# In the wide stages of an fp32r kernel, h_hi and h_lo pass a loaded block of weights side by side, in one 512-column matmul

## The chip, the cores and the metric

The kernel runs on one NeuronCore of a Trainium2 chip (trn2). The metric is the device time of one execution in microseconds (us). The kernel before takes 2521.66 us, the median of 3 runs (2519.83 to 2523.13).

## The reference

The program is a whole small model in fp32 on 256 tokens of width 2048: one block with a mixer (attention, gating and an RWKV recurrence), a cross attention to a memory and a convolved feed-forward, then two layers with three kinds of attention each. What matters here are its projections, all of which are products of 256 rows `h` with a weight matrix:

```python
def hybrid_mixer(h, ...):
    z = h @ w_in                       # 2048 -> 3*768 + 2*512 + 2688 columns
    ...
def conv_ffn(h, w_up, conv_w, conv_b, w_down):
    up = h @ w_up                      # 2048 -> 2*5632
    up_pad = jnp.pad(up, ((0, 0), (CONV_WIDTH - 1, 0), (0, 0)))
    conv = conv_b + sum(up_pad[:, j:j + s] * conv_w[j] for j in range(CONV_WIDTH))
    gate, val = jnp.split(conv, 2, axis=-1)
    return (jax.nn.gelu(gate, approximate=True) * val) @ w_down
```

## The kernel before, in words

**Three products for one.** TensorE takes fp32 data in a reduced form, fp32r, which is faster than plain fp32. To keep the precision, both operands are split into a high part that fp32r holds exactly and the rest: `h = h_hi + h_lo`, `w = w_hi + w_lo`. A product is then `h_hi w_hi + h_hi w_lo + h_lo w_hi`, three matmuls that add up in one region of PSUM (`three_pass`, lines 378 to 381).

**Stages, groups, units.** Each projection is a `Stage`. It is worked in groups of 512 output columns, and a group in 4 units: a unit is 4 blocks of 128 rows of the weights by 512 columns (1 MB). SyncE loads a unit into one of four `raw` slots (`load_units`, L301 and L303). ScalarE copies it rounded into one of two `w_hi` slots (`split_hi`, L316), VectorE writes the difference into `w_lo` (`split_lo`, L321), and TensorE multiplies (`multiply`). `split_hi` of a unit waits until the unit two before it has been used (`unit_used`), and the next load into a `raw` slot waits for `lo_made`.

**Two forms.** A stage with `tok` makes the tokens the output rows: a 128x128 block of h is loaded as weights and 512 columns of w stream past it. A stage with `ch` makes the channels the output rows: a 128x128 block of w is loaded and the 256 tokens of h stream past it. For each of 4 blocks c of 128 channels and each of the unit's 4 blocks k of rows there are three matmuls of 256 columns: w_hi past h_hi (L379), then w_hi past h_lo (L380), then w_lo past h_hi (L381), 48 in a unit. In the trace the operand that streams is written first: `PS<-h_lo,w_hi` streams h_lo past w_hi. The `ch` stages that the change touches are `ST_C` (4 groups), `ST_CE` (1 group of 3 blocks of channels), `ST_UP` (22 groups, the feed-forward's first half) and the `q` stage of each of the two last layers (2 groups each). The other `ch` stages (`mem_k`, half of `bc`, `qk`, `mem_q`, half of `kv`, `c_qk`) stay as they are.

**Banks.** PSUM has 8 banks of 512 columns. A group takes two of them, and two groups in a row take different pairs. The first matmul of a group waits for the evacuation of the group two before it.

**Evacuation and what follows.** While TensorE works on a group, ScalarE and VectorE take the sums of the group before out of PSUM, right after they have split the new group's unit 1 (`evac_scalar`, `evac_vector`). In `ST_UP` the evacuation is the convolution itself: ScalarE multiplies each of 4 blocks by the tap of the same token and adds the bias, PSUM to SBUF (`up_scalar`, L1603); VectorE adds the two taps of earlier tokens, 8 instructions that read PSUM (`up_vector`, L1615). After the new group's unit 3 come the gelu (L1622) and the product with the other half (L1626). `ST_UP` is followed by `ST_DOWN`, whose stationary operand is this result (`act_ff`): its first unit needs the last group of `ST_UP` to be through all these steps and split again (L1674, L1681).

**Order.** All engines' orders are written out by hand; there is no scheduler. `ST_UP` runs in hardware loops of two groups a turn.

Of the kernel before, what the change touches and what calls it, by code (L numbers as in the profile page):

```python
# [14 lines left out]
P = 128  # L15
# [56 lines left out]
class Stage:  # L72


    def __init__(self, count, name, src, groups, tok=None, ch=None, n_cols=512, units=4, kb=4):
# [6 lines left out]
        self.scalar_end = self.vector_end = None  # L82

# [3 lines left out]
    def parity(self, g):  # L87
        return (self.G + g) % 2


# [37 lines left out]
def hybrid_two_blocks(nc, I, out):  # L128

    with ExitStack() as ctx:  # L130
        def sb(name, shape, dt=F32):
            return ctx.enter_context(nc.sbuf_tensor(name, shape, dt))
# [53 lines left out]
        def col(n):  # L186
# [13 lines left out]
        SW, SBIAS = 21248, 22272  # L200
        CONV = 16128
        cat = ar(CAT, TB, D)
# [16 lines left out]
            new(n) for n in ("hi_made", "lo_made", "unit_used", "act_evac", "dve_evac", "squared", "gained"))  # L219
        taps, gelu_made, gated_made, ff_hi, ff_lo = (  # L220
            new(n) for n in ("taps", "gelu_made", "gated", "ff_hi", "ff_lo"))
        (mem_in, consts_in, rel_in, rel_out, rel_back, x_in, sgu_in, masks_in, lora_in, g_up_in, ln_in, gains_in,
# [7 lines left out]
        def w_cols(w, col0, stride=512, n_cols=512):  # L230
# [10 lines left out]
        ST_BC = Stage(count, "bc", w_cols(w_in, 3 * A_W + 768), 1, tok=(0, 256), ch=(256, 256))  # L241
        ST_C = Stage(count, "c", w_cols(w_in, C0 + 256), 4, ch=(0, 512))
        ST_CE = Stage(count, "c_end", w_cols(w_in, C0 + 256 + 2048, n_cols=384), 1, ch=(0, 384), n_cols=384)
        ST_VB = Stage(count, "vb", w_cols(w_in, 2 * A_W + 512), 1, tok=(0, 512))
# [6 lines left out]
        ST_UP = Stage(count, "ffn_up", lambda g, j: tuple(w_up[:, 4 * j:4 * j + 4, bass.ds(g * S + a, S)]  # L251
                                                          for a in (0, D_FF)), FB // 2, ch=(0, 512))
        ST_DOWN = Stage(count, "ffn_down", lambda q, j: w_down[:, bass.ds(q * 4 + j, 1), :], FB // 4, kb=1, n_cols=2048)
        count["group"] = ST_DOWN.G
        ST2 = []
        for layer in range(LAYERS):
            w = I["w_in_2"][layer]
            ST2.append(dict(
                q=Stage(count, "q", w_cols(w, 0), 2, ch=(0, 512)),
                kv=Stage(count, "kv", w_cols(w, 1024), 1, tok=(256, 256), ch=(0, 256)),  # L260
                tok=Stage(count, "tok", w_cols(w, 1536), 4, tok=(0, 512)),
                tok_end=Stage(count, "tok_end", w_cols(w, 3584, n_cols=192), 1, tok=(0, 192), n_cols=192),
                c_qk=Stage(count, "c_qk", w_cols(w, 3776), 2, ch=(0, 512)),
                c_vg=Stage(count, "c_vg", w_cols(w, 4800), 2, tok=(0, 512)),
                out=Stage(count, "w_out_2", w_cols(I["w_out_2"][layer], 0), 4, tok=(0, 512))))
# [66 lines left out]
        def group_scalar(act, q, before=None, made=0):  # L332
            st = q.st
            for j in range(st.units):
                if j >= made:
                    split_hi(act, q, j)
                if j == min(1, st.units - 1) and before is not None:
                    evac_scalar(act, before)
                yield
            if before is not None and before.st.scalar_end:  # L340
                before.st.scalar_end(act, before)

        def group_vector(dve, q, before=None, made=0):
            st = q.st
            for j in range(st.units):
                if j >= made:
                    split_lo(dve, q, j)
                if j == min(1, st.units - 1) and before is not None:
                    evac_vector(dve, before)
                yield  # L350
            if before is not None and before.st.vector_end:
                before.st.vector_end(dve, before)

        def last_scalar(act, q):
            evac_scalar(act, q)
# [82 lines left out]
        def to_tokens(st, dst, col0):  # L438
            plain_evac(st, lambda g: dst[:, 0, bass.ds(g * 512 + col0, 512)],
                       lambda g: dst[:, 1, bass.ds(g * 512 + col0, 512)])  # L440

        def to_channels(st, at, blk0):
            plain_evac(st, lambda g: arena[:, bass.ds(g * 1024 + (at + blk0 * S), 512)],
                       lambda g: arena[:, bass.ds(g * 1024 + (at + blk0 * S + 512), 512)])
# [11 lines left out]
        to_channels(ST_C, Z_C, 2)  # L456
        plain_evac(ST_CE, lambda g: ar(Z_C + 18 * S, 512), lambda g: ar(Z_C + 20 * S, 256))

# [1132 lines left out]
        act_ff = ar(0, FB * S)  # L1591
        conv = ar(CONV, 2, 4, S)

# [4 lines left out]
        def up_scalar(act, q):  # L1598
            if q.c >= 2:
                act.wait_ge(gated_made, q.plus(2, q.c - 1))  # L1600
            for m in range(4):
                half, c = m // 2, m % 2
                last = act.activation(conv[:, q.parity, m, :], PS[:, 2 * q.parity + half, c * S:(c + 1) * S], ACT.Identity,  # L1603
                                      scale=channel("conv_w", q.g, half, c, 2), bias=channel("conv_b", q.g, half, c))
            last.then_inc(act_evac, 1)

        def up_vector(dve, q):
            dve.wait_ge(act_evac, q.number(1))
            for back in (1, 2):
                if back == 2:  # L1610
                    dve.wait_ge(taps, q.plus(2, q.c + 1))
# [6 lines left out]
                last.then_inc(taps if back == 1 else dve_evac, 1)  # L1618

        def gate_scalar(act, q):  # L1620
            act.wait_ge(dve_evac, q.number(1))
            act.activation(conv[:, q.parity, 0:2, :], conv[:, q.parity, 0:2, :], ACT.Gelu_apprx_tanh).then_inc(gelu_made, 1)  # L1622

        def gate_vector(dve, q):
# [1026 lines left out]
```

## Time and profile before

| | |
|---|---|
| runs | 2519.83, 2521.66, 2523.13 us |
| the profiled execution's own time | 2520.95 us |
| its span, first to last instruction | 2519.2 us |
| TensorE (matmul) busy | 2316.0 us, 92% of the span, 14998 matmuls |
| VectorE busy | 1324.6 us, 53% |
| ScalarE busy | 1020.8 us, 41% |
| mean granted TensorE clock | 0.954 of full speed |
| share of TensorE in the chain that ended last | 87% |

A matmul's busy time in the profile (284 ns for 256 columns) is from its start to the modelled end of its pipeline, and the next one starts before that. What a matmul costs in a stream is the distance between two starts, read in the timeline, or the length of a stretch over the number of matmuls in it.

### The profile page before, as it was taken

The page shows a single profiled execution, that of the slowest core. Times are in us where ns is not written, and L with a number is a line of the kernel's source. Part 1 is how long each engine was busy: PE and PEld are TensorE (multiplying, and loading weights), DVE is VectorE, ACT ScalarE, POOL GpSimd, SP SyncE. Part 2 cuts the span into 40 slices and gives each one's busy share as a digit, 9 for nine tenths or more (in the row PEclk, how much of TensorE's full clock was granted, in tenths as well). Part 3 has the DMA queues.
Part 4 walks back from the last instruction along what each step waited for, and adds up shares of the span by engine and source line. Part 5 has one row for each costly group of instructions (what it writes and reads, how often), then busy time and mean ns, then how long its engine had stood idle before and what let it go on. Part 6 is the DMA issues. An engine that isn't in the chain of part 4 may idle for free.

```text
span 2519.2 us, 35800 instructions
## 1 busy us (share of the span) xinstructions
PE 2316.0 (92%) x14998; PEld 2097.8 (83%) x14998; DVE 1324.6 (53%) x1675; ACT 1020.8 (41%) x1303; POOL 44.4 (2%) x55
## 2 busy tenths in 40 slices
PE   7999987978888899999998999799998999999897
PEld 6898976867766899999997888698976779898676
DVE  5444645375555655555554554644455554444654
ACT  4433432322444544444443344433444343343542
POOL 0000010010000000000000000000000000000000
PEclk9999987979899999999999999899998999999898
DMA  7456520000643455555554555364640446555033
GB/s 283 153 170 213 182 78 1 1 1 11 227 164 101 150 184 181 181 181 181 181 198 161 188 199 187 129 224 156 206 134 1 151 159 221 183 186 167 1 122 129
DMA packets 217831, 373.12 MB, mean 148 GB/s; under 512 B 8263, under 2 KB 108020, under 8 KB 210804
## 3 DMA queue, kind: packets, MB, share of 16 engines
q1 hardware_dynamic: 211088, 360.48, 42.7%
q10 hardware_dynamic: 6628, 10.98, 1.2%
q8 instruction: 87, 1.43, 0.2%
q14 instruction: 28, 0.23, 0.0%
HBM read 369.32 MB, written 2.12 MB: 147 GB/s over the span
## 4 chain that ended last, share of the span: by engine, by line
PE 87%; DVE 8%; ACT 3%; DMA 1%; issue 1%; POOL 0%; ACTq 0%; DVEq 0%; SPq 0%
PE PS L379 25%; PE PS L381 25%; PE PS L380 25%; PE PS L1509 2%; PE PS L996 1%; DVE w_lo L321 1%; PE PS L1493 1%; PE PS L1003 1%; DVE small L1546 1%; ACT w_hi L316 1%; DVE spare L1542 1%; PE PS L574 1%; PE PS L1332 1%; PE PS L1331 1%; DVE x L659 1%
## 5 line engine op out<-in xcount | busy, mean ns | idle before, releaser
L321 DVE TENSOR_TENSOR w_lo<-raw,w_hi 128x2048 fp32r<-128x2048 f32 (+2 forms) x340 | 766.4, 2254 | 786.7 <-ACT w_hi L316 784.7
L316 ACT ACTIVATE w_hi<-raw 128x2048 fp32r<-128x2048 f32 (+2 forms) x340 | 640.3, 1883 | 772.3 <-PE PS L381 755.3
L379 PE MATMUL PS<-h_hi,w_hi 128*128 128x256 f32 x2640 | 750.3, 284 | 5.8 <-DVE w_lo L321 3.6
L381 PE MATMUL PS<-h_hi,w_lo 128*128 128x256 f32 x2640 | 747.9, 283 | 0.0
L380 PE MATMUL PS<-h_lo,w_hi 128*128 128x256 f32 x2640 | 747.9, 283 | 0.0
L379 PE MATMUL PS<-w_hi,h_hi 128*128 128x512 f32 (+2 forms) x1440 | 551.4, 383 | 35.1 <-DVE h_lo L596 12.0
L381 PE MATMUL PS<-w_hi,h_lo 128*128 128x512 f32 (+2 forms) x1440 | 548.1, 381 | 0.0
L380 PE MATMUL PS<-w_lo,h_hi 128*128 128x512 f32 (+2 forms) x1440 | 548.0, 381 | 0.0
L379 PEld LDWEIGHTS PS<-h_hi,w_hi 128*128 128x128 f32 x2640 | 507.2, 192 | 7.7 <-issue 3.9
L380 PEld LDWEIGHTS PS<-h_lo,w_hi 128*128 128x128 f32 x2640 | 507.3, 192 | 0.0
L381 PEld LDWEIGHTS PS<-h_hi,w_lo 128*128 128x128 f32 x2640 | 507.2, 192 | 0.0
L379 PEld LDWEIGHTS PS<-w_hi,h_hi 128*128 128x128 f32 x1440 | 274.7, 191 | 87.5 <-issue 18.9
L381 PEld LDWEIGHTS PS<-w_hi,h_lo 128*128 128x128 f32 x1440 | 274.2, 190 | 50.9
L380 PEld LDWEIGHTS PS<-w_lo,h_hi 128*128 128x128 f32 x1440 | 274.5, 191 | 50.1
L574 PE MATMUL PS<-ident,arena 128*128 128x128 f32 x296 | 46.9, 319 | 63.7 <-ACT arena L533 36.8
L574 PEld LDWEIGHTS PS<-ident,arena 128*128 128x128 f32 x296 | 42.0, 168 | 68.2 <-issue 36.0
L1615 DVE SCALAR_TENSOR_TENSOR arena<-PS,params,arena 128x255 f32<-128x255 f32 (+1 forms) x176 | 72.6, 474 | 6.2 <-ACT arena L1603 3.5
L1674 ACT ACTIVATE h_hi<-arena 128x256 fp32r (+1 forms) x44 | 18.3, 418 | 139.5 <-PE PS L381 138.8
L581 ACT ACTIVATE h_hi<-PS,params 128x256 fp32r<-128x256 f32 x106 | 42.4, 474 | 62.9 <-PE PS L574 62.7
L525 POOL TENSOR_TENSOR small<-small 128x2 f32<-128x2 f32 (+2 forms) x31 | 27.2, 885 | 2035.9 <-DVE small L656 955.2
L591 DVE SCALAR_TENSOR_TENSOR h_lo<-PS,params,h_hi 128x256 fp32r<-128x256 f32 x106 | 43.8, 476 | 33.1 <-ACT h_hi L581 33.1
L1681 DVE TENSOR_TENSOR h_lo<-arena,h_hi 128x256 fp32r<-128x256 f32 x44 | 18.6, 425 | 64.2 <-ACT h_hi L1674 64.2
(466 smaller groups left out, 1652.3 us busy)
## 6 DMA issues: line engine op xcount, KB each, us to landing
raw<-in_w_in SPq DMA_DIRECT2D x132, 1024.0 KB, 5.1
raw<-in_ffn_w_up SPq DMA_DIRECT2D x176, 512.0 KB, 4.3
raw<-in_w_out SPq DMA_DIRECT2D x48, 1024.0 KB, 5.1
raw<-in_ffn_w_down SPq DMA_DIRECT2D x44, 1024.0 KB, 4.7
raw<-in_mem_wkv SPq DMA_DIRECT2D x8, 1024.0 KB, 7.2
raw<-in_mem_wq SPq DMA_DIRECT2D x4, 1024.0 KB, 5.1
raw<-in_mem_wo SPq DMA_DIRECT2D x4, 1024.0 KB, 5.5
raw<-in_w_in SPq DMA_DIRECT2D x4, 768.0 KB, 4.5
```

Of the source, the lines that this page charges most:

```text
L316: act.activation(w_hi[:, slot % 2, :st.n], raw[:, slot, :st.n], ACT.Copy).then_inc(hi_made, 1)
L321: dve.tensor_tensor(w_lo[:, slot % 2, :st.n], raw[:, slot, :st.n], w_hi[:, slot % 2, :st.n].bitcast(F32), ALU.subtract).then_inc(lo_made, 1)
L379: pe.matmul(ps, l_hi, r_hi, start=start, stop=False, skip_group_check=skip)
L380: pe.matmul(ps, l_hi, r_lo, start=False, stop=False, skip_group_check=skip)
L381: return pe.matmul(ps, l_lo, r_hi, start=False, stop=stop, skip_group_check=skip)
L525: return pool.tensor_tensor(c, c, minus_half.to_broadcast([P, n]), ALU.pow)
L574: last = pe.transpose(PS[:, turn_bank(n), at:at + P], block(t, k), ident[:, :])
L581: act.activation(h_hi[:, k, :], PS[:, turn_bank(n), (k % 2) * S:(k % 2 + 1) * S], ACT.Copy, scale=gain(k)).then_inc(j.act, 1)
L591: dve.scalar_tensor_tensor(out=h_lo[:, k, :], in0=PS[:, turn_bank(n), (k % 2) * S:(k % 2 + 1) * S], scalar=gain(k), in1=h_hi[:, k, :].bitc ...
L659: dve.scalar_tensor_tensor(out=x[:, tb, :], in0=y[:, tb, :], scalar=j.rstd[:, tb:tb + 1], in1=x[:, tb, :], op0=ALU.mult, op1=ALU.add).then ...
L1509: last = pe.matmul(PS[:, bank, t_ * P:(t_ + 1) * P], s_[:, (kb * TB + t_) * P:(kb * TB + t_ + 1) * P], job["v"][:, kb, :], start=kb == 0, ...
L1615: last = dve.scalar_tensor_tensor(out=d, in0=PS[:, 2 * q.parity + half, c * S:(c + 1) * S - back], scalar=channel("conv_w", q.g, half, c, ...
```

## The change

For the stages with the new argument `wide`, one matmul streams h_hi and h_lo, 256 columns each, past a block of w_hi. Its 512 results fill one PSUM bank: `h_hi w_hi` in the left half, `h_lo w_hi` in the right half. The matmul with w_lo adds into the left half. A unit's block of channels has its four wide matmuls first, then its four with w_lo. For this h_hi and h_lo become two halves of one tensor `h_both`, a group takes four banks (0 to 3 or 4 to 7 in turn), and the evacuation adds the halves: ScalarE copies the left halves of the banks to SBUF, and VectorE adds the right halves to them in place. In `ST_UP` the sums land in a new buffer `rows_up`, and the convolution reads that, one unit later (`scalar_mid`, `vector_mid`, after unit 2).

```diff
-        h_hi = sb("h_hi", [P, KB, S], F32R)
-        h_lo = sb("h_lo", [P, KB, S], F32R)
+        h_both = sb("h_both", [P, 2, KB, S], F32R)
+        h_hi, h_lo = h_both[:, 0], h_both[:, 1]
...
+    def wide_bank(self, g):
+        return (self.wide + 4 * g) % 8
...
+        ST_C = Stage(..., ch=(0, 512), wide=4)
+        ST_CE = Stage(..., ch=(0, 384), n_cols=384, wide=4)
+        ST_UP = Stage(..., ch=(0, 512), wide=0)
+                q=Stage(count, "q", w_cols(w, 0), 2, ch=(0, 512), wide=0),
...
@@ group_scalar (group_vector alike)
                 if j == min(1, st.units - 1) and before is not None:
                     evac_scalar(act, before)
+                if j == 2 and before is not None and before.st.scalar_mid:
+                    before.st.scalar_mid(act, before)
@@ multiply
-                pe.wait_ge(act_evac, q.number(-1))
-                pe.wait_ge(dve_evac, q.number(-1))
+                late = 0 if st.wide == 0 and q.c == 0 and q.i is None else -1
+                pe.wait_ge(act_evac, q.number(late))
+                pe.wait_ge(dve_evac, q.number(late))
...
-            if st.ch:
+            if st.wide is not None:
+                c0, n = st.ch
+                for c in range(n // P):
+                    cs = slice(c0 + c * P, c0 + (c + 1) * P)
+                    sums = PS[:, q.bank + c, :].rearrange("p (a n) -> p a n", a=2)
+                    for k in range(st.kb):
+                        kk = j * st.kb + k
+                        pe.matmul(sums, wh[:, k, cs], h_both[:, :, kk, :], start=kk == 0, stop=False, skip_group_check=True)
+                    for k in range(st.kb):
+                        kk = j * st.kb + k
+                        last = pe.matmul(sums[:, 0, :], wl[:, k, cs], h_hi[:, kk, :], start=False, stop=kk == end,
+                                         skip_group_check=True)
+            elif st.ch:
@@ evacuation of ST_C, ST_CE and q
+        def wide_sums(q, half, c0=0, n=4):
+            return PS[:, q.bank + c0:q.bank + c0 + n, half * S:(half + 1) * S]
+        def wide_evac(st, dst):
+            n = st.ch[1] // P
+            def scalar(act, q):
+                act.activation(blocks_in(dst(q.g), n), wide_sums(q, 0, 0, n), ACT.Copy).then_inc(act_evac, 1)
+            def vector(dve, q):
+                d = blocks_in(dst(q.g), n)
+                dve.wait_ge(act_evac, q.number(1))
+                dve.tensor_tensor(d, d, wide_sums(q, 1, 0, n), ALU.add).then_inc(dve_evac, 1)
@@ evacuation and convolution of ST_UP
         def up_scalar(act, q):
             if q.c >= 2:
                 act.wait_ge(gated_made, q.plus(2, q.c - 1))
+            act.activation(rows_up[:, q.parity, :, :], wide_sums(q, 0), ACT.Copy).then_inc(act_evac, 1)
+
+        def up_vector(dve, q):
+            dve.wait_ge(act_evac, q.number(1))
+            up = rows_up[:, q.parity, :, :]
+            dve.tensor_tensor(up, up, wide_sums(q, 1), ALU.add).then_inc(dve_evac, 1)
+
+        def conv_scalar(act, q):
+            act.wait_ge(dve_evac, q.number(1))
             for m in range(4):
-                last = act.activation(conv[...], PS[:, 2 * q.parity + half, c * S:(c + 1) * S], ACT.Identity,
+                last = act.activation(conv[...], rows_up[:, q.parity, m, :], ACT.Identity,
...
-            last.then_inc(act_evac, 1)
+            last.then_inc(first_tap, 1)
+        def conv_vector(dve, q):
+            dve.wait_ge(first_tap, q.plus(2, q.c + 1))
...
-                    last = dve.scalar_tensor_tensor(out=d, in0=PS[:, 2 * q.parity + half, c * S:(c + 1) * S - back],
+                    last = dve.scalar_tensor_tensor(out=d, in0=rows_up[:, q.parity, m, :S - back],
...
         def gate_scalar(act, q):
-            act.wait_ge(dve_evac, q.number(1))
+            act.wait_ge(taps, q.plus(4, 2 * q.c + 2))
```

How the instructions move, at three places. First TensorE at the start of a unit in the loop of `ST_UP`, before:

```order
3574 L388 ISA
3575 L379 MATMUL PS<-h_hi,w_hi 128x256
3576 L380 MATMUL PS<-h_lo,w_hi 128x256
3577 L381 MATMUL PS<-h_hi,w_lo 128x256
3578 L379 MATMUL PS<-h_hi,w_hi 128x256
```

and of the change (L428 is the wide matmul, L431 the one with w_lo):

```order
2654 L406 ISA
2655 L428 MATMUL PS<-h_both,w_hi 128x512 x4
2656 L431 MATMUL PS<-h_both,w_lo 128x256 x4
2657 L428 MATMUL PS<-h_both,w_hi 128x512 x4
2658 L431 MATMUL PS<-h_both,w_lo 128x256 x4
```

A unit's 48 matmuls of 256 columns (16 times the three lines) have become 16 of 512 and 16 of 256 columns.

Second ScalarE from the first group of `ST_UP` into the second, before (L316 is `split_hi`, L1603 the convolution out of PSUM, L1622 the gelu):

```order
299 L316 ACTIVATE w_hi<-raw 128x2048 x3
300 L1603 ACTIVATE arena<-PS,params 128x256 x4
301 L316 ACTIVATE w_hi<-raw 128x2048 x2
302 L1622 ACT_TABLE_LOAD
303 L1622 ACTIVATE arena<-arena 128x512
```

and of the change (L325 is `split_hi`, L1654 the copy out of PSUM, L1665 the convolution from SBUF, L1684 the gelu):

```order
299 L325 ACTIVATE w_hi<-raw 128x2048 x3
300 L1654 ACTIVATE arena<-PS 128x1024
301 L325 ACTIVATE w_hi<-raw 128x2048
302 L1665 ACTIVATE arena<-arena,params 128x256 x4
303 L325 ACTIVATE w_hi<-raw 128x2048
304 L1684 ACT_TABLE_LOAD
305 L1684 ACTIVATE arena<-arena 128x512
```

The convolution has moved behind one more split, and a copy of 1024 columns stands in its place.

Third ScalarE at the end of `ST_UP`, where nothing lies between the steps, before:

```order
356 L316 ACTIVATE w_hi<-raw 128x2048
357 L1603 ACTIVATE arena<-PS,params 128x256 x4
358 L1622 ACTIVATE arena<-arena 128x512
359 L1674 ACTIVATE h_hi<-arena 128x256 x2
```

and of the change:

```order
366 L325 ACTIVATE w_hi<-raw 128x2048
367 L1654 ACTIVATE arena<-PS 128x1024
368 L1665 ACTIVATE arena<-arena,params 128x256 x4
369 L1684 ACTIVATE arena<-arena 128x512
370 L1737 ACTIVATE h_both<-arena 128x256 x2
```

The chain from the last matmul of `ST_UP` to the first of `ST_DOWN` has one more link on ScalarE, and VectorE has one more too (its addition of 1024 columns, before its 8 taps).

## Rows read from the trace of the kernel before

**Rows 1.** The page: busy shares and the chain that ended last, by engine and line.

```profile
PE 2316.0 (92%) x14998; PEld 2097.8 (83%) x14998; DVE 1324.6 (53%) x1675; ACT 1020.8 (41%) x1303; POOL 44.4 (2%) x55
PE 87%; DVE 8%; ACT 3%; DMA 1%; issue 1%; POOL 0%; ACTq 0%; DVEq 0%; SPq 0%
```

**Rows 2.** Busy us (count) by engine, clock, DMA share, GB/s: ST_C/ST_CE, ST_UP, ST_DOWN, tok.

```profile
99.50:211.70 112.20, 112.20 (x937) 112.20 (x936) 48.02 (x26) 39.03 (x25) 0.00 (x0) 1.00 0.56 183
843.60:1338.90 495.30, 495.30 (x4130) 495.30 (x4129) 278.93 (x279) 216.44 (x196) 0.00 (x0) 1.00 0.56 184
...
1347.30:1589.00 241.70, 241.70 (x1055) 199.96 (x1056) 116.46 (x86) 94.73 (x85) 0.00 (x0) 0.99 0.53 187
...
1681.20:1768.25 87.05, 87.05 (x386) 72.11 (x385) 37.74 (x20) 31.51 (x20) 0.00 (x0) 1.00 0.53 170
```

**Rows 3.** Timeline (start us, us) of TensorE in ST_UP, 256 columns each.

```profile
1000.18 0.28 PE L381 MATMUL PS<-h_hi,w_lo 128*128 128x256 f32 x1
1000.30 0.28 PE L379 MATMUL PS<-h_hi,w_hi 128*128 128x256 f32 x1
1000.42 0.28 PE L380 MATMUL PS<-h_lo,w_hi 128*128 128x256 f32 x1
1000.54 0.28 PE L381 MATMUL PS<-h_hi,w_lo 128*128 128x256 f32 x1
```

**Rows 4.** Timeline of TensorE in a tok stage, 512 then 192 columns each.

```profile
1700.25 0.39 PE L379 MATMUL PS<-w_hi,h_hi 128*128 128x512 f32 x1
1700.48 0.39 PE L380 MATMUL PS<-w_lo,h_hi 128*128 128x512 f32 x1
...
1768.56 0.27 PE L379 MATMUL PS<-w_hi,h_hi 128*128 128x192 f32 x1
...
1768.90 0.27 PE L379 MATMUL PS<-w_hi,h_hi 128*128 128x192 f32 x1
```

**Rows 5.** ScalarE and VectorE through one group of ST_UP (timeline).

```profile
1206.79 1.91 ACT L316 ACTIVATE w_hi<-raw 128x2048 fp32r<-128x2048 f32 x1 [2.03 <-PE PS L381]
...
1205.18 3.44 DVE L1615 SCALAR_TENSOR_TENSOR arena<-PS,params,arena 128x255 f32<-128x255 f32 x8
1208.73 2.29 DVE L321 TENSOR_TENSOR w_lo<-raw,w_hi 128x2048 fp32r<-128x2048 f32 x1
1214.49 2.29 DVE L321 TENSOR_TENSOR w_lo<-raw,w_hi 128x2048 fp32r<-128x2048 f32 x1 [3.47 <-ACT w_hi L316]
```

**Rows 6.** Groups by form: two of 1024 or 512 columns on ScalarE and VectorE.

```profile
L1859 ACT ACTIVATE arena<-arena 128x1024 f32<-128x1024 f32 x6 | 6.3, 1047 | 0.0
L1818 DVE TENSOR_TENSOR x<-x,PS 128x512 f32<-128x512 f32 x8 | 5.5, 683 | 12.0 <-PE PS L381 12.0
```

**Rows 7.** The chain of waits from the last matmul of ST_UP to ST_DOWN's first.

```profile
1339.11 0.13 PE PS L381
1339.26 1.94 ACT arena L1603 x4
1341.29 1.66 DVE arena L1615 x4
1342.98 1.66 DVE arena L1615 x4
1344.67 0.64 ACT arena L1622
1345.33 0.70 DVE arena L1626
1346.06 0.43 ACT h_hi L1674
1346.57 0.44 DVE h_lo L1681
1347.01 0.25 issue
1347.26 0.76 PE PS L379
```

**Rows 8.** Stretches as in rows 2: the start of ST_DOWN, and a plain fp32 matmul (L2101).

```profile
1347.30:1352.60 5.30, 5.30 (x13) 4.14 (x14) 2.33 (x2) 1.28 (x1) 0.00 (x0) 0.50 0.14 20
...
1920.90:1924.30 3.40, 3.40 (x6) 1.37 (x5) 0.00 (x0) 2.95 (x7) 0.00 (x0) 0.50 0.00 0
```

**Rows 9.** Plain fp32 matmuls: L2101 in the timeline, then the lines L2101 and L2089 (ns min/median/max).

```profile
1920.92 3.62 PE L2101 MATMUL PS<-arena 128*128 128x512 f32 x4
...
L2101 PE MATMUL PS<-arena x16: 592/878/1062, 1920.9 to 2385.2; 128*128 128x512 f32 x16
...
L2089 PE MATMUL PS<-arena x80: 378/380/635, 1882.8 to 2364.0; 128*128 128x256 f32 x80
```

More of the change, by code:

```diff
@@ L72, with __init__ @@
 class Stage:
-    def __init__(self, count, name, src, groups, tok=None, ch=None, n_cols=512, units=4, kb=4):
+    def __init__(self, count, name, src, groups, tok=None, ch=None, n_cols=512, units=4, kb=4,
+                 wide=None):
         self.name, self.src, self.groups, self.tok, self.ch = name, src, groups, tok, ch
@@ L81, in __init__ @@
         self.U1, self.G1 = count["unit"], count["group"]
-        self.scalar_end = self.vector_end = None
+        self.wide = wide
+        self.scalar_mid = self.vector_mid = self.scalar_end = self.vector_end = None
     def unit(self, g):
@@ L219, in hybrid_two_blocks @@
             new(n) for n in ("hi_made", "lo_made", "unit_used", "act_evac", "dve_evac", "squared", "gained"))
-        taps, gelu_made, gated_made, ff_hi, ff_lo = (
-            new(n) for n in ("taps", "gelu_made", "gated", "ff_hi", "ff_lo"))
+        first_tap, taps, gelu_made, gated_made, ff_hi, ff_lo = (
+            new(n) for n in ("first_tap", "taps", "gelu_made", "gated", "ff_hi", "ff_lo"))
         (mem_in, consts_in, rel_in, rel_out, rel_back, x_in, sgu_in, masks_in, lora_in, g_up_in, ln_in, gains_in,
@@ L241, in hybrid_two_blocks @@
         ST_BC = Stage(count, "bc", w_cols(w_in, 3 * A_W + 768), 1, tok=(0, 256), ch=(256, 256))
-        ST_C = Stage(count, "c", w_cols(w_in, C0 + 256), 4, ch=(0, 512))
-        ST_CE = Stage(count, "c_end", w_cols(w_in, C0 + 256 + 2048, n_cols=384), 1, ch=(0, 384), n_cols=384)
+        ST_C = Stage(count, "c", w_cols(w_in, C0 + 256), 4, ch=(0, 512), wide=4)
+        ST_CE = Stage(count, "c_end", w_cols(w_in, C0 + 256 + 2048, n_cols=384), 1, ch=(0, 384), n_cols=384,
+                      wide=4)
         ST_VB = Stage(count, "vb", w_cols(w_in, 2 * A_W + 512), 1, tok=(0, 512))
@@ L251, in hybrid_two_blocks @@
         ST_UP = Stage(count, "ffn_up", lambda g, j: tuple(w_up[:, 4 * j:4 * j + 4, bass.ds(g * S + a, S)]
-                                                          for a in (0, D_FF)), FB // 2, ch=(0, 512))
+                                                          for a in (0, D_FF)), FB // 2, ch=(0, 512), wide=0)
         ST_DOWN = Stage(count, "ffn_down", lambda q, j: w_down[:, bass.ds(q * 4 + j, 1), :], FB // 4, kb=1, n_cols=2048)
@@ L349, in group_vector @@
                     evac_vector(dve, before)
+                if j == 2 and before is not None and before.st.vector_mid:
+                    before.st.vector_mid(dve, before)
                 yield
@@ L402, in multiply @@
                                           kk == end, at_once)
-            if st.ch:
+            if st.wide is not None:
+                c0, n = st.ch
[10 more added lines that the diff above has]
+            elif st.ch:
                 c0, n = st.ch
@@ L456, in hybrid_two_blocks @@
         to_channels(ST_C, Z_C, 2)
-        plain_evac(ST_CE, lambda g: ar(Z_C + 18 * S, 512), lambda g: ar(Z_C + 20 * S, 256))
+        wide_evac(ST_CE, lambda g: ar(Z_C + 18 * S, 768))
         def vb_scalar(act, q):
@@ L1600, in up_scalar @@
                 act.wait_ge(gated_made, q.plus(2, q.c - 1))
+            act.activation(rows_up[:, q.parity, :, :], wide_sums(q, 0), ACT.Copy).then_inc(act_evac, 1)
[5 more added lines that the diff above has]
+            act.wait_ge(dve_evac, q.number(1))
             for m in range(4):
                 half, c = m // 2, m % 2
-                last = act.activation(conv[:, q.parity, m, :], PS[:, 2 * q.parity + half, c * S:(c + 1) * S], ACT.Identity,
+                last = act.activation(conv[:, q.parity, m, :], rows_up[:, q.parity, m, :], ACT.Identity,
                                       scale=channel("conv_w", q.g, half, c, 2), bias=channel("conv_b", q.g, half, c))
-            last.then_inc(act_evac, 1)
-        def up_vector(dve, q):
-            dve.wait_ge(act_evac, q.number(1))
+            last.then_inc(first_tap, 1)
+        def conv_vector(dve, q):
+            dve.wait_ge(first_tap, q.plus(2, q.c + 1))
             for back in (1, 2):
                 if back == 2:
-                    dve.wait_ge(taps, q.plus(2, q.c + 1))
+                    dve.wait_ge(taps, q.plus(4, 2 * q.c + 1))
                 for m in range(4):
@@ L1614, in up_vector @@
                     d = conv[:, q.parity, m, back:]
[L1615 removed]
+                    last = dve.scalar_tensor_tensor(out=d, in0=rows_up[:, q.parity, m, :S - back],
                                                     scalar=channel("conv_w", q.g, half, c, 2 - back), in1=d, op0=ALU.mult,
                                                     op1=ALU.add)
[L1618 removed]
+                last.then_inc(taps, 1)
         def gate_scalar(act, q):
[L1621 removed]
+            act.wait_ge(taps, q.plus(4, 2 * q.c + 2))
             act.activation(conv[:, q.parity, 0:2, :], conv[:, q.parity, 0:2, :], ACT.Gelu_apprx_tanh).then_inc(gelu_made, 1)
@@ L1629, in hybrid_two_blocks @@
         ST_UP.scalar_evac, ST_UP.vector_evac = up_scalar, up_vector
+        ST_UP.scalar_mid, ST_UP.vector_mid = conv_scalar, conv_vector
         ST_UP.scalar_end, ST_UP.vector_end = gate_scalar, gate_vector
```

16 lines of the change are left out of this document (13 added, 3 removed).

## The prediction, made before the change was run

> **What bounds the kernel now.** I read the page first: TensorE is busy 92% of the span, and 87% of the chain that ended last is its own work [rows 1]. So a gain has to come out of TensorE's stream, and what the other engines do costs only where TensorE waits for it. Next I cut the span into stages. In `ST_C` with `ST_CE` and in `ST_UP` TensorE is busy in every microsecond at the full clock (1.00), VectorE 43 to 56% and ScalarE 35 to 44% [rows 2]. There is no wait to remove; only the matmuls themselves can become cheaper. Then the timeline, for what one matmul costs, from start to start: the busy figure of 0.28 us overlaps the next matmul and is not the price. With 256 columns the starts are 120 ns apart [rows 3]; over the whole of `ST_UP`, 495.30 us for 22 x 4 x 48 = 4224 matmuls less the two units' 96 of its opening, 4128, gives 119.99 ns. With 512 columns they are 227 ns apart [rows 4]; over 16 units of 24 matmuls, 87.05 / 384 = 226.7 ns [rows 2].
>
> From 256 to 512 columns the price rises by 106.7 ns, which is 256 columns at 2.4 GHz. So both have the same fixed part: 120.0 - 106.7 = 13.3 ns and 226.7 - 213.3 = 13.4 ns. With 192 columns the starts are (1768.90 - 1768.56) / 3 = 113 ns apart [rows 4], 33 ns over the 80 ns of its columns: below 256 columns another floor shows, at about 111 to 113 ns. The new stream has nothing under 256 columns, so that floor stays out of it.
>
> **The matmuls.** The number of columns stays: 3 x 256 before, 512 + 256 after. What goes is one matmul of three, with its weight load, and so one fixed part. Per pair (block of channels c, block of rows k): before 3 x 120.0 = 360.0 ns, after 226.7 + 120.0 = 346.7 ns, 13.3 ns less. Pairs: `ST_C` 4 groups x 4 units x 16 = 256; `ST_CE` 4 x 12 = 48; `ST_UP` 22 x 4 x 16 = 1408; the two q stages 2 x 2 x 4 x 16 = 256. Together 1968 pairs x 13.3 ns = 26.2 us.
>
> The Trainium skill (TensorE: Matmul & The Clock Gate, "Back-to-back issue gap") gives a matmul N / 2.4 ns plus about 2.5 ns at the warm clock. By that a dropped matmul would be worth 2.5 ns, 4.9 us in all, and the kernel would come to about 2519. The trace has 13.3 ns for the fixed part of fp32r matmuls with a weight load each, at both lengths, and the sum goes by the trace.
>
> **The wide matmul's operand.** No fp32r matmul before streams its operand in two pieces (256 columns of h_hi, then 256 of h_lo 16 KB further on). The nearest row is L2101, in plain fp32, which streams 4 pieces of 128 columns, 256 apart (`ukv4[:, k, :, P:2P]`). At the half clock its four matmuls fill 3.62 us, of which the last one's 1.06 us: (3.62 - 1.06) / 3 = 853 ns each [rows 8, 9], exactly 2 x 512 columns at 1.2 GHz. At the full clock its shortest is 592 ns against 378 ns for L2089, which streams 256 columns in one piece [rows 9]: 214 ns for 256 more columns at two steps a column, again nothing for the pieces. Plain fp32 takes two steps a column, though, so a cost of a piece could hide in it. Bounds: 0 from this row; 33 ns, from the 192-column row, if the second piece behaved like a short matmul; below 0 nothing, since no row shows a 512-column matmul under 227. I take 0, the nearest row's.
>
> **The supply of a unit.** A unit of `ST_UP` shrinks from 48 x 0.12 = 5.76 us to 16 x 0.3467 = 5.55 us. Splitting it takes 1.91 + 2.29 us one after the other, started when the unit before the one running is used up [rows 5]; TensorE needs it 5.55 us later, so some 1.2 us are left. The extra work goes into that: after unit 1 ScalarE copies 1024 columns, 1.05 us by L1859 [rows 6], and VectorE adds 1024, which lies between 683 ns for 512 columns [rows 6] and 2290 ns for 2048 [rows 5], so about 1.22 us. Behind ScalarE's copy stands only the split of unit 2, due at 5.55 us, and ScalarE is done at 3.0 us; VectorE is done at 1.94 + 2.29 + 1.22 = 5.45 us, and its next split can start only at 5.55 + 1.94. After unit 2 VectorE's split ends at 4.2 us and ScalarE's four convolution steps at 1.91 + 1.94 = 3.85 us [rows 5, 7]; the 8 taps, 3.44 us [rows 5], run to 7.65 us, and the split of unit 3 that is queued behind them could have started at 7.49. It is 0.16 us late, ends at 9.9, and is needed at 11.1. Cover stays, and TensorE doesn't wait. SyncE's next load, which waits for that split, slips by the same 0.16 us of a three-unit lead. The loads rise from 184 to 191 GB/s, against 187 in `ST_DOWN`, which is busy throughout as well [rows 2]. In `ST_C` and q the copy and the addition are the same and nothing follows them.
>
> The waits on evacuated banks have the same distance of two groups; the `late` wait at the head of `ST_UP` and q is for a group whose sums the opening itself already needed. Both at 0.
>
> **Where it costs.** At the end of `ST_UP` nothing covers. From 1339.11 to 1347.26 us TensorE waits for ScalarE's convolution, VectorE's taps, gelu, product and split, 8.15 us [rows 7]. The change puts the copy (1.05) and the addition (1.22) in front: +2.3 us, all on the path. The taps from SBUF rather than PSUM I leave at their price. After the gap the clock is at 0.50 for the first 5.3 us of `ST_DOWN` [rows 8], which costs 2.65 us; where in the idle time the clock falls and returns differs from gap to gap, so this and the other gaps can move the end by about 2 us either way. At the hand-over from `ST_CE` the split is late already and a unit shorter by 0.16 us adds 0.16. In three openings a split is made in between transposes; I allow 0.2 us in all.
>
> **Sum.** 26.2 - 2.3 - 0.16 - 0.2 = 23.5 us. The profiled execution took 2520.95 us, so 2497.4; that execution lies 0.7 us under the median, which gives 2498.2. I say 2498 us.
>
> **Rivals.**
> *Each piece pays.* If the fixed 13.3 ns belongs to a run of columns and not to a matmul, the wide one takes 240 ns, the pair 360, nothing is gained and the longer tail stays: 2521.7 + 2.7 = 2524. For it: no fp32r row in pieces. Against: L2101 in four pieces. A measurement of this kernel tells 0.2%, 5 us, from no change, so this reads as no change. 0.10.
>
> *A break between the pieces costs more* (the slower side). The price is the short matmul's: 33 ns a wide matmul, so the pair takes 380 ns, 19.7 ns more than now, x 1968 = +38.8, with the tail 2563 us. It loses by 5 us from 14.5 ns a break on ((13.3 x 1968 + 2300) / 1968). Against it speaks the same row L2101, whose 853 ns leave room for 0 ns. 0.06. The Trainium skill (Advanced Engine Details and Errata, "PSUM Cachelines") says that any non-contiguous access pattern slows matmuls significantly, and would put this rival first; but it also says that two neighbours suffice, and here the PSUM side is one run of 512 and the SBUF side runs of 1 KB. L2101's rows disagree with the sweeping form.
>
> *Half comes through.* The break between the pieces costs half of a fixed part, 6.65 ns x 1968 = 13.1 us, or a waiting split inside `ST_UP` gives back as much (0.15 us in each of its 88 units): 2511. For it: the unseen operand, and VectorE's fuller queue. Against: the 1.2 us of cover. 0.07.
>
> *More comes off.* If the fixed part is a clash of a weight load with the stream that a thinner sequence avoids, every matmul of the pair drops to its columns: 213.3 + 106.7 = 320, 40 ns a pair, 79 us, 2445. Against: the 512-column stream has weight loads just as thin and pays 13.4 ns. 0.05.
>
> Forecast 0.72. Its own range, from the clock's 2 us and 1 ns a pair: 2493 to 2504. The range of 8 in 10 takes in the half case: 2490 to 2512. Faster by over 0.2% (under 2516.6): 0.72 + 0.07 + 0.05 = 0.84; within: 0.10; slower: 0.06.
>
> **What would show it.** In the changed profile: starts 227 ns after a wide matmul and 120 ns after one with w_lo; a group of `ST_UP` in 22.2 us instead of 23.05, so the stage 18.7 us shorter; `ST_C` with `ST_CE` 4.0 us shorter; each q stage 1.7; about 10.4 us of idle TensorE before `ST_DOWN` instead of 8.15; no wait for w_lo inside `ST_UP`. I am wrong if the distance after a wide matmul is not 227, or if TensorE shows waits for VectorE in the loop.

## The result and the profile after

The changed kernel takes 2508.13 us (median of 5 runs, 2502.02 to 2510.02) against 2520.63 us before (5 runs, 2519.83 to 2523.13): ratio 0.9939, 95% interval 0.9925 to 0.9954. It is faster by 12.5 us, about half of the 23.5 us that were forecast. It lies in the stated range (2490 to 2512), but outside the forecast's own one (2493 to 2504).

The page of the changed kernel, in the form of [rows 1]:

```profile
PE 2299.9 (92%) x13030; PEld 1994.4 (80%) x13030; DVE 1353.4 (54%) x1697; ACT 1050.4 (42%) x1325; POOL 44.4 (2%) x55
PE 86%; DVE 9%; ACT 3%; DMA 1%; issue 1%; POOL 0%; ACTq 0%; DVEq 0%; SPq 0%
```

1968 matmuls are gone from the 14998, and TensorE bounds the kernel as before. The same stretches as in [rows 2] and [rows 8]: `ST_C` with `ST_CE`; the loop of `ST_UP`; the wait before `ST_DOWN`; `c_qk` of both layers; the start of `ST_DOWN`. The first line can't be set against that of [rows 2] as it stands: the window there also holds 24 matmuls of the stage before `ST_C`, 2.9 us.

```profile
103.90:210.55 106.65, 106.65 (x610) 93.17 (x608) 48.54 (x25) 40.72 (x25) 0.00 (x0) 1.00 0.58 187
841.68:1324.55 482.87, 482.87 (x2755) 421.97 (x2753) 302.06 (x300) 241.20 (x217) 0.00 (x0) 1.00 0.58 189
1324.55:1335.23 10.68, 0.17 (x2) 0.03 (x1) 5.93 (x12) 4.93 (x9) 0.00 (x0) 0.63 0.30 98
1767.84:1816.11 48.27, 48.27 (x391) 48.27 (x392) 22.54 (x25) 22.38 (x24) 1.39 (x2) 0.97 0.53 175
2221.03:2269.39 48.36, 48.36 (x391) 48.36 (x392) 22.54 (x25) 22.38 (x24) 1.39 (x2) 0.96 0.53 174
1335.23:1341.00 5.77, 5.77 (x14) 4.51 (x15) 2.37 (x2) 1.32 (x1) 0.00 (x0) 0.50 0.10 23
```

The loop of `ST_UP` is 86 units, 1376 pairs: 482.87 / 1376 = 350.9 ns a pair where 346.7 were expected and 360.0 stood before (the other two units of the 88 are worked in the stage's opening). TensorE is busy in all of it, so the missing 4 ns are not a wait. The timeline of the changed kernel in that loop shows where they are (start us, us of the merged matmuls):

```profile
1000.39 1.09 PE L428 MATMUL PS<-h_both,w_hi 128*128 128x512 f32 x4
1001.32 0.64 PE L431 MATMUL PS<-h_both,w_lo 128*128 128x256 f32 x4
1001.79 0.40 PE L428 MATMUL PS<-h_both,w_hi 128*128 128x512 f32 x1
```

Four wide matmuls fill 1001.32 - 1000.39 = 0.93 us, 232.5 ns each; four with w_lo 0.47 us, 117.5 each. Over that loop, mean from start to start: a wide one followed by a wide one 233.6 ns, a wide one followed by a w_lo one 228.4, a w_lo one 118.5. (Over the whole trace the first is 234.4, with the stages' openings in it; the texts on the experiments below use that.) A pure stream of 512 columns had 226.7 [rows 2], a pure one of 256 had 120.0.

From span to span (2519.2 to 2507.8, 11.4 us less): `ST_UP` 12.65 less, `ST_C` and `ST_CE` 2.8, the q stages 1.1 each, together 17.7; the wait before `ST_DOWN` 2.5 more; `c_qk` 1.4 and 1.5 more, where the changed kernel's clock is at half for about 3.4 us and before's was not; 0.9 more in the other gaps and restarts together. Of the 12.1 us that these 11.4 fall short of the 23.5 forecast, 8.5 are the matmuls, 2.9 the clock in `c_qk`, 0.2 the wait before `ST_DOWN` and 0.5 the rest.

### The profile page after: what moved, and what is told of

Its sections match the earlier page's. It is cut to its first block, busy times and chain, and to the rows that moved or that the text cites. A ratio compares the mean times of both kernels' runs of the same rounds, so it can differ in the third digit from the quotient of the medians.

```text
span 2507.8 us, 31953 instructions
## 1 busy us (share of the span) xinstructions
PE 2299.9 (92%) x13030; PEld 1994.4 (80%) x13030; DVE 1353.4 (54%) x1697; ACT 1050.4 (42%) x1325; POOL 44.4 (2%) x55
## 4 chain that ended last, share of the span: by engine, by line
PE 86%; DVE 9%; ACT 3%; DMA 1%; issue 1%; POOL 0%; ACTq 0%; DVEq 0%; SPq 0%
PE PS L428 18%; PE PS L396 16%; PE PS L397 16%; PE PS L398 16%; PE PS L431 9%; PE PS L1562 2%; DVE w_lo L330 1%; PE PS L1049 1%; PE PS L1546 1%; DVE small L1599 1%; ACT w_hi L325 1%; PE PS L1056 1%; DVE spare L1595 1%; PE PS L627 1%; PE PS L1385 1%
## 5 line engine op out<-in xcount | busy, mean ns | idle before, releaser
L325 ACT ACTIVATE w_hi<-raw 128x2048 fp32r<-128x2048 f32 (+2 forms) x340 | 640.6, 1884 | 728.6 <-PE PS L398 369.8
L396 PE MATMUL PS<-w_hi,h_both 128*128 128x512 f32 (+2 forms) x1440 | 551.6, 383 | 38.6 <-DVE h_both L649 12.0
L397 PE MATMUL PS<-w_lo,h_both 128*128 128x512 f32 (+2 forms) x1440 | 548.4, 381 | 0.0
L398 PE MATMUL PS<-w_hi,h_both 128*128 128x512 f32 (+2 forms) x1440 | 548.3, 381 | 0.0
L428 PE MATMUL PS<-h_both,w_hi 128*128 128x512 f32 x1968 | 538.3, 395 | 1.5 <-DVE h_both L644 1.5
L428 PEld LDWEIGHTS PS<-h_both,w_hi 128*128 128x128 f32 x1968 | 336.5, 189 | 47.5 <-DVE h_both L644 2.4
L396 PEld LDWEIGHTS PS<-w_hi,h_both 128*128 128x128 f32 x1440 | 275.1, 191 | 91.1 <-issue 22.4
L431 PEld LDWEIGHTS PS<-h_both,w_lo 128*128 128x128 f32 x1968 | 302.0, 189 | 41.9
L398 PEld LDWEIGHTS PS<-w_hi,h_both 128*128 128x128 f32 x1440 | 274.6, 191 | 51.5
L397 PEld LDWEIGHTS PS<-w_lo,h_both 128*128 128x128 f32 x1440 | 274.9, 191 | 50.0
L431 PE MATMUL PS<-h_both,w_lo 128*128 128x256 f32 x1968 | 313.0, 281 | 0.0
L396 PE MATMUL PS<-h_both,w_hi 128*128 128x256 f32 x672 | 193.4, 288 | 4.1 <-DVE w_lo L330 3.6
L397 PE MATMUL PS<-h_both,w_hi 128*128 128x256 f32 x672 | 191.7, 285 | 0.0
L398 PE MATMUL PS<-h_both,w_lo 128*128 128x256 f32 x672 | 191.6, 285 | 0.0
L396 PEld LDWEIGHTS PS<-h_both,w_hi 128*128 128x128 f32 x672 | 130.6, 194 | 5.2 <-issue 3.9
L397 PEld LDWEIGHTS PS<-h_both,w_hi 128*128 128x128 f32 x672 | 130.5, 194 | 0.0
L398 PEld LDWEIGHTS PS<-h_both,w_lo 128*128 128x128 f32 x672 | 130.5, 194 | 0.0
L1677 DVE SCALAR_TENSOR_TENSOR arena<-arena,params 128x255 f32<-128x255 f32 (+1 forms) x176 | 73.2, 478 | 4.9 <-ACT arena L1665 2.1
```

The costliest lines, as they stand in the source:

```text
L325: act.activation(w_hi[:, slot % 2, :st.n], raw[:, slot, :st.n], ACT.Copy).then_inc(hi_made, 1)
L396: pe.matmul(ps, l_hi, r_hi, start=start, stop=False, skip_group_check=skip)
L397: pe.matmul(ps, l_hi, r_lo, start=False, stop=False, skip_group_check=skip)
L398: return pe.matmul(ps, l_lo, r_hi, start=False, stop=stop, skip_group_check=skip)
L428: pe.matmul(sums, wh[:, k, cs], h_both[:, :, kk, :], start=kk == 0, stop=False, skip_group_check=True)
L431: last = pe.matmul(sums[:, 0, :], wl[:, k, cs], h_hi[:, kk, :], start=False, stop=kk == end, skip_group_check=True)
```

## The experiments

**Is it the two pieces, the order or the bank?** The first theory was the break in the streamed operand, the prediction's own doubt. The rivals: the order (a wide matmul right behind a wide one) and the shared PSUM bank.

e1, h_hi and h_lo of a block side by side:

```diff
-        h_both = sb("h_both", [P, 2, KB, S], F32R)
-        h_hi, h_lo = h_both[:, 0], h_both[:, 1]
+        h_both = sb("h_both", [P, KB, 2, S], F32R)
+        h_hi, h_lo = h_both[:, :, 0, :], h_both[:, :, 1, :]
```

The wide matmul, and the instructions that fill h_both, address it accordingly.

> The layout alone: h_both is [KB, 2, S] instead of [2, KB, S], so that h_hi and h_lo of one block of rows lie side by side and the wide matmul streams 512 columns in one piece. Order as in the change (four wide, then four w_lo). In the profile of the change a wide matmul that a wide one follows takes 234.4 ns and one that a w_lo one follows 228.4 ns; w_lo ones 118.5 ns. Theory A (a break in the streamed operand costs about 7 ns): wide to wide falls to 227, a block's eight matmuls from 1405 to about 1382 ns, ST_UP is 352 x 0.023 = 8 us shorter, 2500 us. Theory B (it is the order: a wide matmul right behind a wide one): wide to wide stays at 234, time as the change, 2508 us.

e2, one loop over k instead of two:

```diff
                         pe.matmul(sums, wh[:, k, cs], h_both[:, :, kk, :], ...)
-                    for k in range(st.kb):
-                        kk = j * st.kb + k
                         last = pe.matmul(sums[:, 0, :], wl[:, k, cs], h_hi[:, kk, :], ...)
```

> The order alone: in each block of channels wide, w_lo, wide, w_lo, ... for the four k, layout as in the change (two pieces). Theory B: no wide matmul follows a wide one, so the pair takes 228.4 + 118.4 = 346.8 ns, 4.6 ns less than the change's 351.4; over 1968 pairs 9 us, 2499 us. Theory A: each wide matmul keeps its break, 234 + 119 = 353 ns a pair, time as the change or 3 us above it, 2508 to 2511 us.

e3, both edits:

> Layout of e1 and order of e2 together. Both theories: 227 + 119 to 120 = 346 to 347 ns a pair, about 2499 us. If each of the two has a part of its own, this one is faster than either alone.

e4, k outside, blocks of channels inside:

```diff
+                for k in range(st.kb):
+                    kk = j * st.kb + k
+                    for c in range(n // P):
+                        cs, sums = block(c)
+                        pe.matmul(sums, wh[:, k, cs], h_both[:, :, kk, :], ...)
+                    for c in range(n // P):
+                        cs, sums = block(c)
+                        last = pe.matmul(sums[:, 0, :], wl[:, k, cs], h_hi[:, kk, :], ...)
```

> Layout as in the change, the order within a unit turned: k outside, blocks of channels inside, so for each k four wide matmuls into four different PSUM banks, then four w_lo ones into the four banks. The share of wide matmuls that follow a wide one is as in the change. Theory C (two wide matmuls in a row into the same PSUM bank cost 7 ns): wide to wide falls to 227 or 228, about 2500 us. Theories A and B: stays at 234, about 2508 us.

All three theories fell. The loop of `ST_UP` in e1, in e2, in e3 and in e4:

```profile
841.47:1324.35 482.88, 482.88 (x2755) 421.94 (x2753) 302.14 (x300) 241.12 (x217) 0.00 (x0) 1.00 0.58 189
...
837.66:1323.94 486.28, 486.28 (x2755) 421.60 (x2753) 302.87 (x300) 241.29 (x217) 0.00 (x0) 1.00 0.57 188
...
837.61:1323.90 486.29, 486.29 (x2755) 421.45 (x2753) 302.88 (x300) 241.31 (x217) 0.00 (x0) 1.00 0.57 188
...
841.73:1324.62 482.89, 482.89 (x2755) 421.94 (x2753) 302.11 (x300) 241.22 (x217) 0.00 (x0) 1.00 0.58 189
```

In one piece the loop takes 482.88 us, as in two (482.87): the break is free. Alternating, it is 3.4 us longer, 353.4 ns a pair: a wide matmul then takes 236.5 ns and a w_lo one 116.9. Both edits together (e3) are as e2. With four banks (e4) the loop is as the change's, and wide to wide stays at 233.6 in it. As whole kernels: e1 2510.13 us (ratio 0.9947, 0.9934 to 0.996), e2 2509.05 (0.9943, 0.9928 to 0.9958), e3 2508.42 (0.9948, 0.9935 to 0.9961), e4 2510.78 (0.9953, 0.9938 to 0.9967); their intervals overlap the change's.

**Is it the mixture of lengths or the roles?** What the four had in common was 512- and 256-column matmuls in one stream (theory D), and weights of w under a stream of 512 columns of h (theory E).

e5, no short matmul left in the wide stages:

```diff
-                        last = pe.matmul(sums[:, 0, :], wl[:, k, cs], h_hi[:, kk, :], start=False, ...)
+                        last = pe.matmul(sums, wl[:, k, cs], h_both[:, :, kk, :], start=False, ...)
```

> The change with the w_lo matmul wide as well: it streams h_hi and h_lo past w_lo, so the fourth product h_lo w_lo is added into the right half of the sums, which the reference's precision doesn't need. No 256-column matmul is left in the wide stages. Theory D (the 7 ns come from long and short matmuls in one stream): all starts are 227 apart as in the tok stages, 454 ns a pair, ST_UP 1408 x 0.454 = 639 us. Theory E (they come from the roles: weights of w loaded, 512 columns of h streamed): all starts 234 apart, 468 ns a pair, ST_UP 659 us. Whole kernel 2508 + 1968 x 0.103 to 0.117 = 2711 to 2738 us.

e6, a unit's 16 wide matmuls, then its 16 short ones:

```diff
                 for c in range(n // P):
...
                     for k in range(st.kb):
...
                         pe.matmul(sums, wh[:, k, cs], h_both[:, :, kk, :], ...)
+                for c in range(n // P):
...
                     for k in range(st.kb):
...
                         last = pe.matmul(sums[:, 0, :], wl[:, k, cs], h_hi[:, kk, :], ...)
```

> A unit's 16 wide matmuls first (all four blocks of channels), then its 16 with w_lo: one change of length a unit instead of four. In the change wide to wide is 234.4 ns, wide to w_lo 228.4, w_lo 118.5. Theory D: long runs come near the pure streams, 227 and 120, 347.5 ns a pair, ST_UP 489 us. Theory E: 15 x 234.4 + 228.4 + 16 x 118.5 = 5640 ns a unit, 352.5 ns a pair, ST_UP 496 us as in the change, time 2508 to 2510 us.

e7, short matmuls put among the long ones of the `tok` stages:

```diff
             pe.matmul(ps, l_hi, r_hi, start=start, ...)
-            pe.matmul(ps, l_hi, r_lo, ...)
+            for a in (0, 256):
+                pe.matmul(ps[:, a:a + 256], l_hi, r_lo[:, a:a + 256], ...)
             return pe.matmul(ps, l_lo, r_hi, stop=stop, ...)
```

Only the `tok` stage of each of the last two layers takes this form.

> The change, and in the four tok groups of each of the last two layers the middle one of the three 512-column matmuls (h_hi past w_lo) split into two of 256 columns. There the roles are the other way round (weights of h, columns of w), and pure 512-column streams take 226.7 ns. Theory D: the 512-column matmuls rise to 230 to 236 ns once shorter ones stand among them. Theory E: they stay at 227 and the halves take 120, so the tok stage goes from 86.8 to 86.8 + 128 x 0.0133 = 88.5 us.

e8, before again:

> The kernel before once more, unchanged, for a second profile of it. In the first one the clock stays full in c_qk of both layers (46.87 us each); in the change's profile it is at half for 3.2 to 3.4 us there (48.3 us each). If that drop is the change's, this profile shows 46.87 twice; if it is chance, one of them may show 48.3 here too. Its wide stages' matmuls stay 120 ns apart, its gap before ST_DOWN 8.3 us.

Theory D holds at all three places. The loop of `ST_UP` in e5 and in e6, then both `tok` stages in e7:

```profile
877.56:1501.45 623.89, 623.89 (x2755) 516.59 (x2753) 303.31 (x300) 238.81 (x217) 0.00 (x0) 1.00 0.45 146
...
841.25:1320.19 478.94, 478.94 (x2755) 423.20 (x2753) 301.68 (x300) 241.36 (x217) 0.00 (x0) 1.00 0.58 191
...
1669.89:1758.97 89.08, 89.08 (x514) 77.76 (x513) 37.76 (x20) 31.54 (x20) 0.00 (x0) 1.00 0.52 166
2122.89:2211.90 89.01, 89.01 (x514) 77.69 (x513) 37.76 (x20) 31.54 (x20) 0.00 (x0) 1.00 0.52 166
```

e5: 623.89 / 2752 matmuls = 226.7 ns, the pure stream's price to the tenth, with the operand in two pieces and the roles of the change; the one run took 2712.12 us, where theory D gave 2711 and theory E 2738. e7: the `tok` stage holds the roles of [rows 2] and takes 89.0 us instead of 87.05. The total alone hardly tells the theories apart (E gave 88.5); the single distances do. Its timeline:

```profile
1700.33 0.40 PE L399 MATMUL PS<-w_hi,h_both 128*128 128x512 f32 x1
1700.56 0.39 PE L396 MATMUL PS<-w_hi,h_both 128*128 128x512 f32 x1
1700.79 0.40 PE L398 MATMUL PS<-w_lo,h_both 128*128 128x256 f32 x2
1701.03 0.40 PE L399 MATMUL PS<-w_hi,h_both 128*128 128x512 f32 x1
```

Over the stage its long matmuls take 233 ns (227 before) and the short ones 115 (one run, 2511.47 us). In e6 two neighbouring runs of the loop read

```profile
1002.89 3.82 PE L429 MATMUL PS<-h_both,w_hi 128*128 128x512 f32 x16
1006.54 2.08 PE L434 MATMUL PS<-h_both,w_lo 128*128 128x256 f32 x16
1008.46 2.23 PE L429 MATMUL PS<-h_both,w_hi 128*128 128x512 f32 x9
```

3.65 / 16 = 228.1 ns and 1.92 / 16 = 120 ns. From start to start the first five wide ones of a run take about 233, 236, 228, 233 and 231 ns and all later ones 227; the first short one takes 113, the second 119 and the rest 120. So in runs this long a change from short to long costs some 27 ns, spread over five matmuls, of which the change back returns 7: 20 ns a cycle. Shorter runs pay less for a cycle but have more of them. In the change's runs of four the wide ones take 234, 234, 232.5 and 228 ns and the short ones 117.5 to 119.5, which is 16.5 ns a cycle, four times a unit; alternating (e2) it is 6.6 ns, sixteen times.

e6 as a whole takes 2500.46 us (4 runs; ratio 0.9904, 0.9888 to 0.9921), and again as e11 2502.14 us (0.9923, 0.991 to 0.9937). The second interval overlaps the change's (0.9925 to 0.9954) at its edge. What parts the two kernels clearly is the trace: the loop of `ST_UP` is 3.9 us shorter than the change's in e6 and in e11.

The trace of the kernel before shows the same surcharge, at the few places where a `ch` stage's 256-column matmuls meet a `tok` stage's 512-column ones. The timeline there:

```profile
46.55 0.28 PE L381 MATMUL PS<-h_hi,w_lo 128*128 128x256 f32 x1
46.67 0.40 PE L379 MATMUL PS<-w_hi,h_hi 128*128 128x512 f32 x1
...
47.83 0.39 PE L381 MATMUL PS<-w_hi,h_lo 128*128 128x512 f32 x1
```

From 46.67 to 47.83 us lie five 512-column matmuls: 1.16 us, 232 ns each, where a pure stream takes 1.13. One by one they are 233, 236, 229, 233 and 231 ns, then 226; the same series stands at 1681.18 and 2134.08 us. Where 256-column matmuls follow 512-column ones (255.81 us), the first takes 113 and the second 119.

e8 (2524.71 us, one run) shows one thing more, `c_qk` in both layers:

```profile
1784.29:1831.16 46.87, 46.87 (x392) 46.87 (x392) 22.54 (x25) 22.39 (x24) 1.39 (x2) 1.00 0.55 181
2235.67:2284.03 48.36, 48.36 (x392) 48.36 (x392) 22.55 (x25) 22.39 (x24) 1.40 (x2) 0.96 0.54 175
```

It took 46.87 us in one layer and 48.36 in the other, where the clock was at half for 3.4 us. The drop that the change's profile shows there happens without the change. It is part of what scatters these runs by several us.

**The price around the matmuls, and a better kernel.** e10 keeps everything of the change but its matmuls:

```diff
-                        pe.matmul(sums, wh[:, k, cs], h_both[:, :, kk, :], start=kk == 0, ...)
-                    for k in range(st.kb):
-                        kk = j * st.kb + k
+                        pe.matmul(sums[:, 0, :], wh[:, k, cs], h_hi[:, kk, :], start=kk == 0, ...)
+                        pe.matmul(sums[:, 1, :], wh[:, k, cs], h_lo[:, kk, :], start=False, ...)
                         last = pe.matmul(sums[:, 0, :], wl[:, k, cs], h_hi[:, kk, :], start=False, ...)
```

> All of the change but its point: layout, banks, evacuation, convolution a unit later, and for each pair still three 256-column matmuls (w_hi past h_hi into the left half, w_hi past h_lo into the right, w_lo past h_hi into the left). It prices what the change adds around the matmuls. If that is the tail before ST_DOWN alone: ST_UP at 508.6 us, ST_C 92.0, the gap 10.8 instead of 8.3 us, 2.5 us above before. If the fuller ScalarE and VectorE queues cost something inside the stages, ST_UP is above 508.7.

e9 turns every second unit of e6 round and halves the last evacuation of `ST_UP`:

```diff
+                for part in ((wides, lows), (lows, wides))[j % 2]:
+                    last = part()
...
+            if is_last(q):
+                act.activation(rows_up[:, q.parity, 0:2, :], wide_sums(q, 0, 0, 2), ACT.Copy).then_inc(half_act, 1)
+                act.activation(rows_up[:, q.parity, 2:4, :], wide_sums(q, 0, 2, 2), ACT.Copy).then_inc(act_evac, 1)
+                return
```

with the additions and the convolution of that group in the same two halves, and the gelu waiting for the first half alone.

> e6's long runs, and every second unit turned round (w_lo ones first, then the wide ones), so that long runs meet across the border of two units: half a cycle of changes a unit instead of one. If each cycle from short to long and back costs what e6's profile shows (first five wide ones 234, 235, 229, 232, 231 instead of 227, the first short one 113: 21 to 24 ns), 124 units save half of it, 1.4 us. And the evacuation and convolution of the last ST_UP group in two halves, ScalarE and VectorE side by side, which should take about 2 us out of the 10.8 us of waiting before ST_DOWN. Together 3.4 us under e6, 2497 us by e6's 2500.5. If the cost sits in the length of a run or in a unit's border and not in the changes of length, ST_UP stays at 491.9 us.

> e6 unchanged, on the chip and beside the runs of before of e9, so that the two can be compared: ratio to before 0.990 as in its first call, 3.4 us above e9.

The loop of `ST_UP` and the wait before `ST_DOWN`, first of e10, then of e9:

```profile
844.17:1339.60 495.43, 495.43 (x4131) 495.39 (x4129) 303.24 (x300) 240.58 (x217) 0.00 (x0) 1.00 0.56 184
1339.60:1350.28 10.68, 0.17 (x3) 0.04 (x1) 5.93 (x12) 4.93 (x9) 0.00 (x0) 0.66 0.25 93
...
839.92:1318.01 478.09, 478.09 (x2755) 423.23 (x2753) 301.66 (x300) 241.09 (x217) 0.00 (x0) 1.00 0.58 191
1318.01:1326.37 8.36, 0.16 (x1) 0.03 (x1) 6.11 (x13) 5.02 (x10) 0.00 (x0) 0.75 0.34 125
```

e10's loop is 495.43 us, as before (120.0 ns a matmul), and its wait is the change's 10.68: the fuller queues cost nothing inside the stage. As a whole it takes 2522.23 us (10 runs; ratio 1.0004, 0.9995 to 1.0013), not told from before. The 2.5 us, which its trace has, lie within that interval (it ends at 3.3 us): the time neither shows nor refutes them. e9's loop is at 347.4 ns a pair, 0.7 above the pure streams' sum, and its wait is 2.3 us shorter. At 2496.45 us (4 runs; ratio 0.9901, 0.9885 to 0.9916) it has the lowest median of all; e11, on the same chip, took 2502.14, 5.7 us more where 3.4 were expected; the two intervals overlap. e9 makes both edits at once; its trace gives 0.85 us of the loop of `ST_UP` to the order and 2.3 us to the halves. Its profiled execution also gains 3.5 us in the stretch from 317 to about 650 us (332.4 against 335.8), in work that neither edit touches, at a mean clock of 0.85 against 0.84: that part is scatter.

## Why the prediction came out as it did

**The bound and its consequence: right.** In the stretches shown of the wide stages TensorE is busy in every microsecond, before and after, and what its stream loses comes off the end.

**The matmuls: the term that was mis-sized.** "after 226.7 + 120.0 = 346.7 ns, 13.3 ns less", 26.2 us. Measured are 350.9 ns a pair in `ST_UP`, and 17.7 us in all wide stages. The step that failed is taking the price of each length from a pure stream of that length. Right behind short matmuls a long one takes up to 236 ns; e5, e6 and e7 show that it is the change of length. The prediction's own sign of being wrong ("if the distance after a wide matmul is not 227") came true, at 233.6 and 228.4. No row that I had read held the surcharge, but the trace of before did, at 46.67, 1681.18 and 2134.08 us; in [rows 2] and [rows 4], both from inside long streams, it is averaged away or absent.

**The operand in two pieces: right.** I took 0, by L2101; e1 and e5 show 0. The rival *Each piece pays* and the slower one both fall. So does, for the streamed operand, the sweeping form of the rule in the Trainium skill (Advanced Engine Details and Errata, "PSUM Cachelines"): the loop takes 482.87 us in two pieces and 482.88 in one. By the 2.5 ns of the Trainium skill (TensorE: Matmul & The Clock Gate, "Back-to-back issue gap") the kernel would have been at about 2519, an estimate; it is at 2508. That section gives the formula for an isolated matmul, without a budget for its weight load, and here each matmul has one.

**The supply: right.** No wait for w_lo inside `ST_UP`, in the change or in e6, whose units are shorter still (478.94 of 478.94 us busy). The cover was a little larger than I wrote: 5.55 - 4.20 leaves 1.35 us, not 1.2. VectorE's addition took 1214 ns (1.22 us expected), ScalarE's copy 1005 (1.05).

**The tail: right.** 2.3 us were expected, 2.5 came, mostly since ScalarE's four steps were slower from SBUF ([rows 7] had 1.94 us for four; now 2.08). The chain of waits of the changed kernel, in the place of [rows 7]:

```profile
1324.76 1.03 ACT arena L1654
...
1325.88 1.23 DVE arena L1659
...
1327.14 2.08 ACT arena L1665 x4
...
1329.24 1.68 DVE arena L1677 x4
...
1335.23 0.76 PE PS L396
```

**The clock: the 2 us either way were too few.** The forecast looked at gaps alone; `c_qk` at half clock, inside a busy stretch, can move a run by 1.5 us in each layer, and the change's five runs span 8 us: 2502.02 and 2503.25 at a mean clock of 0.956, 2508.13 to 2510.02 at 0.953 to 0.954.

**The rivals.** The time came out near *Half comes through* (2511), but not for its reasons: neither the break nor the split cost anything. So it is partly luck that the time lies in the range, which was widened from 2504 to 2512 for that rival. None of the rivals names what happened: I had the mixture of lengths before me, and priced only its parts. One slip in the working changes nothing: the 14.5 ns of the slower rival come from (13.3 x 1968 - 2660 + 5000) / 1968, and the bracket as written adds the tail instead.

## What to carry to other kernels

A matmul's price read in a stream of its like holds for such a stream. If a change mixes lengths, look in the trace for a place where such matmuls already meet, and read the first ones behind it one by one. Here a cycle cost 6.6 ns alternating, 16.5 in runs of four and about 20 in runs of sixteen, so the sum still falls with longer runs: the same 32 matmuls of a unit took 350.9 ns a pair in runs of four, 353.4 alternating, 348.1 in runs of sixteen and 347.4 in runs across units. Where an evacuation ends in an uncovered wait, halve it, so that two engines work on it side by side; here that took 2.3 of 10.7 us out (e9).

## What the runs showed of the hardware

- After a long run of 256-column fp32r matmuls, 512-column ones took 233, 236, 228, 233, 231 and then 227 ns from start to start, at the full clock: in e6 with h streamed, and in the kernel before with w streamed (233, 236, 229, 233, 231, 226). In runs of four they took about 234, 234, 232 and 228, into one bank (the change) as into four (e4). After a long run of 512-column ones the first of 256 columns took 113 ns, the second 119, then 120. What in TensorE settles over these five matmuls no run shows; it stays open.
- A 512-column operand in two pieces 16 KB apart streams as fast as one in one piece: 226.7 ns each in e5, and e1's loop equals the change's to 0.01 us.
- The clock fell to half for 3.4 us inside `c_qk` in profiles of the kernel before as of others, in the stage's first microseconds, while TensorE was busy again after 1.81 us of idle. The idle time alone does not decide it: it was 1.81 us in both layers of the change and of both profiles of before, and the clock fell in two, none and one of the two layers.
